# Attention of a hybrid decoder step: P·V as split fp32r passes over the full array, and scores head by head

## Chip, cores and metric

The kernel runs on one core of one Trainium2 chip. The metric is the device time of one execution in microseconds (us), the median of several runs.

## What is computed

One inference step of a two-layer decoder trunk in fp32, for 1024 prompt tokens and 8 sample tokens that share all weights. Layer 0 mixes tokens by sliding-window attention (16 query heads of 64, 4 key/value heads, window 128, a sink per head, rotary positions), layer 1 by chunkwise retention. A gated ConvFFN follows each mixer, with a post-layer norm after each part. The change lies in the attention of layer 0 over the prompt, cut here to its core:

```python
qb = q.reshape(b, nb, WINDOW, ATTN_HEADS, ATTN_HEAD_DIM)          # nb = 8 blocks of 128 tokens
s = jnp.einsum('...qkgd,...skd->...kgqs', qg, k) * (ATTN_HEAD_DIM ** -0.5)   # keys: previous and own block
s = jnp.where(valid, s, -jnp.inf)
m = jnp.maximum(jnp.max(s, axis=-1, keepdims=True), sink)
p = jnp.exp(s - m)
w = p / (jnp.sum(p, axis=-1, keepdims=True) + jnp.exp(sink - m))
o = jnp.einsum('...kgqs,...skd->...qkgd', w, v)
out = o.reshape(b, t, ATTN_HEADS * ATTN_HEAD_DIM) @ w_o
```

## The kernel before

Five engines run five programs, in an order written out by hand; semaphores join them. Large matmuls are done in split fp32r: each fp32 operand x is kept as hi (x rounded to fp32r by ACT's copy) and lo (x − hi, by a subtraction on VectorE or POOL). `accumulate` (L476) then does three passes per term: hi·hi, hi·lo, lo·hi. All 1032 token columns (1024 prompt, 8 sample) stay in SBUF, features on partitions.

Attention runs over four head groups g of one kv head and four query heads (GH=4) each. Within a group TensorE (L643) goes through t = 0 to 8, with a software pipeline over the eight blocks b of 128 tokens:

- `project(t)`: q, k, v of block t, 24 passes of 384 columns into bank t%2 (t = 8 is the sample rows).
- `turn(t-1)`: three transposes of q and k (two heads of q per 128 columns; k is there twice, once per array half) into bank 2.
- `values(t-4)`: P·V into bank 7. Two key blocks (one for block 0) times two head parities, plain fp32; parity 0 writes partitions 0 to 63, parity 1 partitions 64 to 127.
- `scores(t-2)`: q·k into banks 3 and 4. Contraction is over 64, so even heads lie in partitions 0 to 63 and odd heads in 64 to 127. The keys hold a ring of three blocks (KR), so the two key blocks are one piece of 256 columns, except in blocks 3 and 6, where they are two pieces of 128; block 0 has one piece of 128.
- `turn_probs(t-3)`: eight transposes of the probabilities into banks 5 and 6.

The output projection `down(q0, q1)` (L626) follows: 24 jobs q of six passes of 344 columns, added into y by VectorE (`add_y`). For q below 8 the banks alternate (q%2), so job q waits for the add of job q−2; from q=8 there are four banks in groups 0 to 2, and in the last group two until q=16. Between them stand the remaining steps of the pipeline: `down(0,4)`, `values(5)`, `scores(7)`, `turn_probs(6)`, `down(4,8)`, the sample rows' scores, `values(6)`, `turn_probs(7)`, `down(8,12)`, `values(7)`, and so on.

ACT, in each t: `v_in(t)` (copy of v out of the bank), `t_hi(t-1)` (hi of q and k), `heads_hi(t-4)`, `pt_in(t-3)` (copy of the transposed probabilities), `exps(t-2)`. VectorE, in each t: `inverse(t-3)` (L1495), `rope(t)` (L1459 to L1461), `t_lo(t-1)` (L1467), `shift(t-2)` (mask and max, L1482), `heads_lo(t-4)` (L1503). POOL: `probs(t-3)` (L1956, the multiply by the inverse sums), `add_rope(t)`. After the loop VectorE interleaves `add_y` (L1403) with the rest.

What is ordered around the change: `t_hi(t-1)` waits for scores(t-2), since it overwrites q; `turn_probs` waits for POOL's `probs`; `values` waits for `pt_in`; `project(b)` waits for `rope(b-2)`, which frees its bank.

Of the kernel before, what the change touches and what calls it, by code (L numbers as in the profile page):

```python
# [12 lines left out]
P = 128  # L13
# [241 lines left out]
def fillers():  # L255
# [10 lines left out]
    for n in range(NB):  # L266
# [14 lines left out]
ATT_SEMS = ("table_in cache_in rope_t v_in v_fp qk back t_hi t_lo score shifted small small2 expd "  # L281
            "inv probs pt pt_in heads heads_hi heads_lo kv_out win_out s_sc s_scc "
# [39 lines left out]
def build(nc, A):  # L322
    ctx = ExitStack()
    with ctx:
# [45 lines left out]
        K.a_v = sb("a_v", [P, VR, HD])  # L370
# [5 lines left out]
        K.a_pt = sb("a_pt", [P, 2, GH * W])  # L376
# [109 lines left out]
def tensor_engine(pe, K):  # L486
# [36 lines left out]
    def attention(g):  # L523
        last = g == NG - 1

        def project(b):
# [6 lines left out]
            if b >= 2:  # L533
                pe.wait_ge(T["rope_t"], (NB + 1) * g + b - 1)
# [24 lines left out]
        def scores(b):  # L559
# [5 lines left out]
            for j in range(2):  # L565
                q = slice(W * j, W * j + W)
                for k0, at, n in pieces:
                    passes = ((K.a_qh, K.a_kh), (K.a_qh, K.a_kl), (K.a_ql, K.a_kh))
                    for n_pass, (qs, ks) in enumerate(passes):
                        for odd in range(2):  # L570
                            r = slice(HD * odd, HD * odd + HD)
                            mm = pe.matmul(bank[3 + odd][:, j * 256 + at:j * 256 + at + n], qs[r, q], ks[r, k0:k0 + n],
                                           start=(n_pass == 0), stop=(n_pass == 2))
            mm.then_inc(T["score"], 1)

        def turn_probs(b):
            pe.wait_ge(T["probs"], NB * g + b + 1)
            if b >= 1:
                pe.wait_ge(T["pt_in"], NB * g + b)
# [5 lines left out]
        def values(b):  # L585
            pe.wait_ge(T["pt_in"], NB * g + b + 1)
            if b >= 1:
                pe.wait_ge(T["heads_lo"], NB * g + b)
            first = 0 if b else 1
            for t in range(first, 2):  # L590
                for odd in range(2):
                    mm = pe.matmul(bank[7][HD * odd:HD * odd + HD, 0:2 * W], K.a_v[:, (b - 1 + t) % VR, :],  # L592
                                   K.a_pt[:, t, :].rearrange("p (j h n) -> p j h n", j=2, h=2)[:, :, odd, :],
                                   start=(t == first), stop=(t == 1))
            mm.then_inc(T["heads"], 1)
# [15 lines left out]
        def sample_turn_probs():  # L611
# [3 lines left out]
            pe.wait_ge(T["pt_in"], NB * (g + 1))  # L615
# [326 lines left out]
def scalar_engine(act, K):  # L942
# [48 lines left out]
    def attention(g):  # L991
        last = g == NG - 1

        def v_in(b):
            act.wait_ge(S["jobs"], J["qkv", g, b])
            if b < NB:
                after(act, T["heads"], NB * g + max(b - 4, 0))
                act.activation(K.a_v[:, b % VR, :], bank[b % 2][:, 320:384], ACT.Copy).then_inc(T["v_in"], 1)
# [23 lines left out]
        def pt_in(b):  # L1022
# [1382 lines left out]
```

## Time and profile before

| | |
|---|---|
| Time, median of 3 runs | 3007.52 us (3007.17 to 3007.52) |
| The profiled execution's own time | 3007.52 us |
| Its span, first to last instruction | 3005.7 us |
| TensorE busy (matmuls) | 2881.6 us, 96% |
| VectorE busy | 1515.3 us, 50% |
| ACT busy | 901.8 us, 30% |
| POOL busy | 584.5 us, 19% |
| Granted TensorE clock, mean | 0.984 |

PE is TensorE's matmuls, PEld its weight loads (both at once are normal), DVE is VectorE, POOL is GpSimd, SP the engine that issues most DMAs. Matmul ends are modelled, so the distance from one start to the next says more than a duration. "x2" in a timeline merges like instructions that follow each other. In the granted clock 1.00 is 2.4 GHz, 0.50 is 1.2 GHz. "Idle before, releaser" is how long an engine stood ahead of an instruction and who ended it; "issue" means that nothing in the profile shows what it waited for. An fp32 matmul shows as more than one record, an fp32r pass as one.

### The profile page before, as it was taken

To read this page: it belongs to the slowest core of one execution; us is meant where nothing else is said; L and a number is where in the kernel's file an instruction comes from. 1 tells how busy PE (TensorE), PEld (TensorE's weight loads), DVE (VectorE), ACT (ScalarE), POOL (GpSimd) and SP (SyncE) were. 2 spreads that over 40 slices of the span, in tenths; PEclk is the share of its full clock that TensorE was granted. 3 is DMA by queue.
4 is the path that set the end of the run, shared out by engine and by line. 5 is a ranking of instruction groups with operands and counts; after the bars stand their busy time and mean duration, and the time that the engine had idled before them with its cause. 6 is when DMAs were issued, how large, how long until landed. Compare 5 with 4: busy or idle time off the path is not lost.

```text
span 3005.7 us, 44058 instructions
## 1 busy us (share of the span) xinstructions
PE 2881.6 (96%) x17996; PEld 2735.8 (91%) x17996; DVE 1515.3 (50%) x3021; ACT 901.8 (30%) x1683; POOL 584.5 (19%) x496
## 2 busy tenths in 40 slices
PE   6999979999999999999999999999999999999996
PEld 6888859999999999998888888888899999999995
DVE  4555566544454444615344354366675454444445
ACT  4344344222211222322433433322152122222113
POOL 1333351000000003403123232111141000000012
PEclk9999989999999999999999999999999999999997
DMA  3200100211111111234555555666411111111101
GB/s 127 75 30 16 43 30 30 70 43 43 43 55 44 43 57 49 75 124 147 174 182 179 165 180 167 218 197 200 152 43 57 43 51 49 43 57 43 43 25 57
DMA packets 192488, 260.48 MB, mean 87 GB/s; under 512 B 29280, under 2 KB 150752, under 8 KB 192256
## 3 DMA queue, kind: packets, MB, share of 16 engines
q1 hardware_dynamic: 126352, 195.64, 20.6%
q10 hardware_dynamic: 65936, 62.03, 6.0%
q8 instruction: 143, 2.34, 0.3%
q14 instruction: 57, 0.47, 0.1%
HBM read 191.50 MB, written 68.20 MB: 86 GB/s over the span
## 4 chain that ended last, share of the span: by engine, by line
PE 83%; issue 6%; DVE 5%; POOL 3%; ACT 2%; SPq 1%; DMA 0%; ACTq 0%; POOLq 0%; DVEq 0%
PE bank L480 26%; PE bank L482 26%; PE bank L481 26%; PE bank L891 2%; ACT y L983 1%; POOL a_prob L1956 1%; PE bank L592 1%; DVE wl L1378 1%; PE bank L518 1%; DVE bank L1425 1%; PE bank L582 1%; PE bank L857 0%; DVE y L1432 0%; POOL a_qk L1945 0%; DVE n_sq L1418 0%
## 5 line engine op out<-in xcount | busy, mean ns | idle before, releaser
L480 PE MATMUL bank<-xh,wh 128*128 128x344 f32 x3648 | 1182.1, 324 | 29.0 <-DVE wl L1378 10.9
L482 PE MATMUL bank<-xh,wl 128*128 128x344 f32 x3648 | 1169.2, 321 | 0.0
L481 PE MATMUL bank<-xl,wh 128*128 128x344 f32 x3648 | 1169.1, 320 | 0.0
L480 PEld LDWEIGHTS bank<-xh,wh 128*128 128x128 f32 x3648 | 689.5, 189 | 57.6 <-issue 20.5
L481 PEld LDWEIGHTS bank<-xl,wh 128*128 128x128 f32 x3648 | 689.1, 189 | 5.2 <-issue 0.2
L482 PEld LDWEIGHTS bank<-xh,wl 128*128 128x128 f32 x3648 | 689.3, 189 | 0.0
L1403 DVE TENSOR_TENSOR y<-bank,y 128x344 f32<-128x344 f32 x648 | 324.8, 513 | 227.6 <-PE bank L482 227.3
L1998 POOL TENSOR_TENSOR f_hl<-f_cv,f_hh 128x344 fp32r<-128x344 f32 x132 | 122.9, 932 | 1276.7 <-ACT f_hh L1100 1276.7
L480 PE MATMUL bank<-f_hh,wh 128*128 128x344 f32 x1056 | 339.8, 322 | 0.0
L482 PE MATMUL bank<-f_hh,wl 128*128 128x344 f32 x1056 | 337.4, 319 | 0.0
L481 PE MATMUL bank<-f_hl,wh 128*128 128x344 f32 x1056 | 337.1, 319 | 0.0
L1378 DVE TENSOR_TENSOR wl<-raw,wh 128x1024 fp32r<-128x1024 f32 x187 | 226.6, 1240 | 159.3 <-ACT wh L953 159.2
L1086 ACT ACTIVATE f_ab<-bank 128x344 f32<-128x344 f32 x132 | 60.2, 456 | 643.8 <-PE bank L482 643.8
L953 ACT ACTIVATE wh<-raw 128x1024 fp32r<-128x1024 f32 x216 | 218.1, 1048 | 69.5 <-PE bank L482 43.3
L1637 DVE TENSOR_TENSOR f_cv<-f_cv,bank 128x344 f32<-128x344 f32 x132 | 67.5, 512 | 300.1 <-PE bank L482 297.9
L481 PEld LDWEIGHTS bank<-f_hl,wh 128*128 128x128 f32 x1056 | 198.5, 188 | 0.6
L480 PEld LDWEIGHTS bank<-f_hh,wh 128*128 128x128 f32 x1056 | 198.5, 188 | 0.6
L482 PEld LDWEIGHTS bank<-f_hh,wl 128*128 128x128 f32 x1056 | 198.6, 188 | 0.0
L1618 DVE TENSOR_SCALAR f_cv<-f_ab,taps 128x344 f32<-128x344 f32 (+1 forms) x132 | 64.0, 485 | 211.2 <-ACT f_ab L1086 211.2
L1100 ACT ACTIVATE f_hh<-f_cv 128x344 fp32r<-128x344 f32 x132 | 64.8, 491 | 311.6 <-DVE f_cv L1637 311.6
L1173 ACT ACTIVATE p_plain<-bank 128x344 f32<-128x344 f32 x96 | 43.9, 457 | 298.0 <-PE bank L482 279.0
L2036 POOL TENSOR_TENSOR r_sl<-r_state,r_sh 128x1024 fp32r<-128x1024 f32 x28 | 66.8, 2386 | 270.9 <-ACT r_sh L1283 270.9
(202 smaller groups left out, 3509.5 us busy)
## 6 DMA issues: line engine op xcount, KB each, us to landing
raw<-in_w SPq DMA_DIRECT2D x216, 512.0 KB, 3.7
scratch_qkvg<-p_plain ACTq DMA_DIRECT2D x96, 172.0 KB, 2.1
r_s<-in_state_in SPq DMA_DIRECT2D x32, 512.0 KB, 3.6
out_state_s<-r_s ACTq DMA_DIRECT2D x32, 512.0 KB, 5.0
scratch_qkvg<-p_rot ACTq DMA_DIRECT2D x24, 344.0 KB, 2.9
r_cxq<-scratch_qkvg SPq DMA_DIRECT2D x32, 256.0 KB, 5.6
r_cxv<-scratch_qkvg SPq DMA_DIRECT2D x32, 256.0 KB, 5.7
r_cxg<-scratch_qkvg SPq DMA_DIRECT2D x32, 256.0 KB, 5.2
```

The source lines that it names most:

```text
L480: pe.matmul(out, ah, bh, start=(k == 0), stop=False)
L481: pe.matmul(out, ah, bl, start=False, stop=False)
L482: mm = pe.matmul(out, al, bh, start=False, stop=(k == n - 1))
L953: act.activation(K.wh[:, SLOT[s], :], K.raw[:, s % RAW, :], ACT.Copy).then_inc(S["hi_done"], 1)
L1086: act.activation(K.ab[:, t % 3, 2 + ch * CH:2 + (ch + 1) * CH], bank[BANK["up", L, t, 0, ch]][:, 0:CH], ACT.Copy)\
L1100: act.activation(K.hh[:, t // 2 % 2, t % 2, columns(ch)], K.cv[:, cv_of(t, ch), :], ACT.Copy).then_inc(S["h_hi"], 1)
L1378: dve.tensor_tensor(K.wl[:, SLOT[s], :], K.raw[:, s % RAW, :], K.wh[:, SLOT[s], :].bitcast(F32), ALU.subtract)\
L1403: dve.tensor_tensor(t, bank[b][:, 0:CH], t, ALU.add).then_inc(S["yadd"], 1)
L1618: x = dve.tensor_scalar(v[:, 0:m], a[:, c0:c0 + m], tap(0), tap(3), ALU.mult, ALU.add)
L1637: dve.tensor_tensor(v, v, bank[BANK["up", L, t, 1, ch]][:, 0:CH], ALU.mult).then_inc(S["gate"], 1)
L1998: pool.tensor_tensor(K.hl[:, t // 2 % 2, t % 2, columns(ch)], v, k.bitcast(F32), ALU.subtract).then_inc(S["h_lo"], 1)
L2036: pool.tensor_tensor(K.sl[:, :, :], K.state[:, :, :], K.sh[:, :, :].bitcast(F32), ALU.subtract).then_inc(R["s_lo"], 1)
```

## The change

P·V becomes a sum of three fp32r products over the full array: ACT's copies `v_hi` and `pt_hi` now write the hi parts (v twice side by side, so that 128 weight columns fill both halves of bank 7), and VectorE makes the lo parts, `v_lo` at the end of `rope` and `pt_lo` as a new step. The result has 512 columns, of which heads_hi and heads_lo read the halves that hold each parity. `scores` now takes head after head, the three passes of a head in a row, in place of alternating even and odd heads within each pass. `project(b)` waits for v_lo (`v_free`) instead of rope's last operation. pt_lo stands last in each t on VectorE, and in the output projection after shift(7) (for block 6) and after sample_shift (for block 7).

```diff
--- before.py
+++ after.py
@@ -367,13 +367,15 @@
         K.sq = sb("n_sq", [P, KT, CH])
 
         sb = place(REGION)
-        K.a_v = sb("a_v", [P, VR, HD])
+        K.a_vh = sb("a_vh", [P, VR, 2, HD], F32R)
+        K.a_vl = sb("a_vl", [P, VR, 2, HD], F32R)
         K.a_vf = sb("a_vf", [P, HD])
         K.a_vs = sb("a_vs", [NS, HD])
         K.a_qk = sb("a_qk", [P, 2, 384])
         K.a_prob = sb("a_prob", [P, GH, 2 * W])
         K.a_st = sb("a_st", [P, 8, GH])
-        K.a_pt = sb("a_pt", [P, 2, GH * W])
+        K.a_pth = sb("a_pth", [P, 2, GH * W], F32R)
+        K.a_ptl = sb("a_ptl", [P, 2, GH * W], F32R)
         K.a_oh = sb("a_oh", [P, 2, TOK], F32R)
         K.a_ol = sb("a_ol", [P, 2, TOK], F32R)
         K.a_sq = sb("a_sq", [HD, 5, NS])
@@ -531,7 +533,7 @@
             if g == 0:
                 pe.wait_ge(S["x_lo"], 1 + sum((b + 1) * W > end for _, end in PIECES[:-1]))
             if b >= 2:
-                pe.wait_ge(T["rope_t"], (NB + 1) * g + b - 1)
+                pe.wait_ge(T["v_free"], NB * g + b - 1)
             o = bank[b % 2][0:m, 0:384].rearrange("m (a n) -> m a n", a=3)
             t = slice(b * W, b * W + m)
             terms = []
@@ -562,37 +564,32 @@
                 pe.wait_ge(T["shifted"], GH * (NB * g + b))
             kb = b % KR * W
             pieces = [(kb, W, W)] if b == 0 else [(kb - W, 0, 2 * W)] if b % KR else [((KR - 1) * W, 0, W), (0, W, W)]
-            for j in range(2):
-                q = slice(W * j, W * j + W)
+            for h in range(GH):
+                r = slice(HD * (h % 2), HD * (h % 2) + HD)
+                q = slice(W * (h // 2), W * (h // 2) + W)
                 for k0, at, n in pieces:
-                    passes = ((K.a_qh, K.a_kh), (K.a_qh, K.a_kl), (K.a_ql, K.a_kh))
-                    for n_pass, (qs, ks) in enumerate(passes):
-                        for odd in range(2):
-                            r = slice(HD * odd, HD * odd + HD)
-                            mm = pe.matmul(bank[3 + odd][:, j * 256 + at:j * 256 + at + n], qs[r, q], ks[r, k0:k0 + n],
-                                           start=(n_pass == 0), stop=(n_pass == 2))
+                    o = bank[3 + h % 2][:, (h // 2) * 256 + at:(h // 2) * 256 + at + n]
+                    mm = accumulate(pe, o, [(K.a_qh[r, q], K.a_ql[r, q], K.a_kh[r, k0:k0 + n], K.a_kl[r, k0:k0 + n])])
             mm.then_inc(T["score"], 1)
 
         def turn_probs(b):
             pe.wait_ge(T["probs"], NB * g + b + 1)
             if b >= 1:
-                pe.wait_ge(T["pt_in"], NB * g + b)
+                pe.wait_ge(T["pt_lo"], NB * g + b)
             for t in range(0 if b else 1, 2):
                 for h in range(GH):
                     mm = pe.transpose(bank[5 + t][:, h * W:(h + 1) * W], K.a_prob[:, h, t * W:(t + 1) * W], ident[:, :])
             mm.then_inc(T["pt"], 1)
 
         def values(b):
-            pe.wait_ge(T["pt_in"], NB * g + b + 1)
+            pe.wait_ge(T["pt_lo"], NB * g + b + 1)
             if b >= 1:
                 pe.wait_ge(T["heads_lo"], NB * g + b)
-            first = 0 if b else 1
-            for t in range(first, 2):
-                for odd in range(2):
-                    mm = pe.matmul(bank[7][HD * odd:HD * odd + HD, 0:2 * W], K.a_v[:, (b - 1 + t) % VR, :],
-                                   K.a_pt[:, t, :].rearrange("p (j h n) -> p j h n", j=2, h=2)[:, :, odd, :],
-                                   start=(t == first), stop=(t == 1))
-            mm.then_inc(T["heads"], 1)
+            terms = []
+            for t in range(0 if b else 1, 2):
+                v = b - 1 + t
+                terms.append((K.a_vh[:, v % VR, :, :], K.a_vl[:, v % VR, :, :], K.a_pth[:, t, :], K.a_ptl[:, t, :]))
+            accumulate(pe, bank[7][:, :], terms).then_inc(T["heads"], 1)
 
         def sample_scores():
             pe.wait_ge(T["t_lo"], (2 * NB + 1) * (g + 1))
...
@@ -991,11 +988,12 @@
     def attention(g):
         last = g == NG - 1
 
-        def v_in(b):
+        def v_hi(b):
             act.wait_ge(S["jobs"], J["qkv", g, b])
             if b < NB:
                 after(act, T["heads"], NB * g + max(b - 4, 0))
-                act.activation(K.a_v[:, b % VR, :], bank[b % 2][:, 320:384], ACT.Copy).then_inc(T["v_in"], 1)
+                act.activation(K.a_vh[:, b % VR, :, :], bank[b % 2][:, 320:384].rearrange("m (a n) -> m a n", a=1)
+                               .to_broadcast([P, 2, HD]), ACT.Copy).then_inc(T["v_hi"], 1)
             if b == NB - 1:
                 after(act, T["kv_out"], 64 * g)
                 act.activation(K.a_vf[:, :], bank[b % 2][:, 320:384], ACT.Copy).then_inc(T["v_fp"], 1)
@@ -1019,12 +1017,12 @@
                                accum_out=K.a_st[:, 4, h:h + 1])
             act.activation(K.a_st[:, 5, :], K.a_st[:, 3, :], ACT.Exp).then_inc(T["expd"], 1)
 
-        def pt_in(b):
+        def pt_hi(b):
             act.wait_ge(T["pt"], NB * g + b + 1)
             after(act, T["heads"], NB * g + b)
             for t in range(0 if b else 1, 2):
-                a = act.activation(K.a_pt[:, t, :], bank[5 + t][:, :], ACT.Copy)
-            a.then_inc(T["pt_in"], 1)
+                a = act.activation(K.a_pth[:, t, :], bank[5 + t][:, :], ACT.Copy)
+            a.then_inc(T["pt_hi"], 1)
 
         def heads_hi(b):
             act.wait_ge(T["heads"], NB * g + b + 1)
@@ -1033,18 +1031,18 @@
             for h in range(2):
                 r = slice(HD * h, HD * h + HD)
                 a = act.activation(K.a_oh[r, :, b * W:(b + 1) * W],
-                                   bank[7][r, 0:2 * W].rearrange("p (j n) -> p j n", j=2), ACT.Copy)
+                                   bank[7][r, :].rearrange("p (j h n) -> p j h n", j=2, h=2)[:, :, h, :], ACT.Copy)
             a.then_inc(T["heads_hi"], 1)
 
         for t in range(NB + 2):
             if t <= NB:
-                v_in(t)
+                v_hi(t)
             if t >= 1:
                 t_hi(t - 1)
             if t >= 4:
                 heads_hi(t - 4)
             if t >= 3:
-                pt_in(t - 3)
+                pt_hi(t - 3)
             if t >= 2:
                 exps(t - 2)
 
...
@@ -1447,7 +1445,7 @@
         def rope(b):
             m = P if b < NB else NS
             if b < NB:
-                dve.wait_ge(T["v_in"], NB * g + b + 1)
+                dve.wait_ge(T["v_hi"], NB * g + b + 1)
             if b >= NB - 1:
                 dve.wait_ge(T["v_fp"], 2 * g + b - NB + 2)
             after(dve, T["qk"], 2 * (NB + 1) * g + (2 * (b - 1) if b >= 2 else 0))
@@ -1460,6 +1458,10 @@
             dve.tensor_tensor(a2[:, :, 1, :], src[:, :, 0, :], sn.to_broadcast([m, 5, 32]), ALU.mult)
             dve.scalar_tensor_tensor(a2[:, :, 0, :], src[:, :, 1, :], -1.0, sn.to_broadcast([m, 5, 32]),
                                      ALU.mult, ALU.mult).then_inc(T["rope_t"], 1)
+            if b < NB:
+                dve.tensor_tensor(K.a_vl[:, b % VR, :, :], bank[b % 2][:, 320:384].rearrange("m (a n) -> m a n", a=1)
+                                  .to_broadcast([P, 2, HD]), K.a_vh[:, b % VR, :, :].bitcast(F32),
+                                  ALU.subtract).then_inc(T["v_free"], 1)
 
         def t_lo(b):
             if b < NB:
@@ -1496,12 +1498,18 @@
             dve.wait_ge(T["small2"], NB * g + b + 1)
             dve.reciprocal(K.a_st[:, 7, :], K.a_st[:, 6, :]).then_inc(T["inv"], 1)
 
+        def pt_lo(b):
+            dve.wait_ge(T["pt_hi"], NB * g + b + 1)
+            for t in range(0 if b else 1, 2):
+                a = dve.tensor_tensor(K.a_ptl[:, t, :], bank[5 + t][:, :], K.a_pth[:, t, :].bitcast(F32), ALU.subtract)
+            a.then_inc(T["pt_lo"], 1)
+
         def heads_lo(b):
             dve.wait_ge(T["heads_hi"], NB * g + b + 1)
             for h in range(2):
                 r = slice(HD * h, HD * h + HD)
                 a = dve.tensor_tensor(K.a_ol[r, :, b * W:(b + 1) * W],
-                                      bank[7][r, 0:2 * W].rearrange("p (j n) -> p j n", j=2),
+                                      bank[7][r, :].rearrange("p (j h n) -> p j h n", j=2, h=2)[:, :, h, :],
                                       K.a_oh[r, :, b * W:(b + 1) * W].bitcast(F32), ALU.subtract)
             a.then_inc(T["heads_lo"], 1)
 
@@ -1564,18 +1572,22 @@
                 shift(t - 2)
             if t >= 4:
                 heads_lo(t - 4)
+            if t >= 3:
+                pt_lo(t - 3)
         t_lo(NB)
         add_y(0, 2)
         inverse(NB - 2)
         add_y(2, 4)
         heads_lo(NB - 3)
         shift(NB - 1)
+        pt_lo(NB - 2)
         add_y(4, 6)
         inverse(NB - 1)
         add_y(6, 8)
         sample_copy()
         heads_lo(NB - 2)
         sample_shift()
+        pt_lo(NB - 1)
         add_y(8, 10)
         sample_probs()
         add_y(10, 12)
```

What is left out renames semaphores in the same way (`v_in` to `v_hi`, `pt_in` to `pt_hi` and `pt_lo`).

## Rows read from the trace of the kernel before

**Rows 1.** The page: the span, and the chain of waits by engine.
```profile
span 3005.7 us, 44058 instructions
...
PE 83%; issue 6%; DVE 5%; POOL 3%; ACT 2%; SPq 1%; DMA 0%; ACTq 0%; POOLq 0%; DVEq 0%
```

**Rows 2.** Busy time by stretch, second group: PE, PEld, DVE, ACT, POOL, clock, DMA.
```profile
115.00:208.00 93.00, 89.18 (x629) 78.55 (x630) 47.73 (x192) 40.42 (x134) 33.84 (x30) 0.98 0.13 47
```

**Rows 3.** TensorE's waits, same group: total us, times, longest.
```profile
PE bank L582 <- POOL a_prob L1956: 1.4, 3, 0.8
PE bank L480 <- DVE y L1403: 1.3, 2, 0.9
```

**Rows 4.** Timeline, TensorE, one block: start, duration, what; PEld is its weight load.
```profile
157.29 0.49 PE L552 MATMUL bank<-ident,a_qk 128*128 128x128 f32 x3
157.71 1.08 PE L592 MATMUL bank<-a_pt,a_v 128*64 128x256 f32 x8
...
158.72 0.19 PEld L572 LDWEIGHTS bank<-a_kh,a_qh 64*128 64x128 f32 x2 [0.38 <-issue]
...
158.88 0.28 PE L572 MATMUL bank<-a_kl,a_qh 64*128 64x128 f32 x2
...
160.00 0.28 PE L572 MATMUL bank<-a_kh,a_ql 64*128 64x128 f32 x2
```

**Rows 5.** Timeline, TensorE, first and last of the 12 passes of one run.
```profile
72.47 0.34 PE L480 MATMUL bank<-wh,xh 128*128 128x384 f32 x1
...
74.39 0.34 PE L482 MATMUL bank<-wh,xl 128*128 128x384 f32 x1
```

**Rows 6.** Timeline, TensorE, scores of block 7: two passes with their loads.
```profile
191.50 0.18 PEld L572 LDWEIGHTS bank<-a_kh,a_qh 64*128 64x128 f32 x2 [0.39 <-issue]
...
191.72 0.28 PE L572 MATMUL bank<-a_kl,a_qh 64*128 64x256 f32 x2
...
192.20 0.29 PE L572 MATMUL bank<-a_kh,a_ql 64*128 64x256 f32 x2
...
192.41 0.31 PEld L582 LDWEIGHTS bank<-ident,a_prob 128*128 128x128 f32 x3
```

**Rows 7.** Groups by line, VectorE: count, busy us, mean ns, idle before.
```profile
L1403 DVE TENSOR_TENSOR y<-bank,y 128x344 f32<-128x344 f32 x648 | 324.8, 513 | 227.6 <-PE bank L482 227.3
L1378 DVE TENSOR_TENSOR wl<-raw,wh 128x1024 fp32r<-128x1024 f32 x187 | 226.6, 1240 | 159.3 <-ACT wh L953 159.2
...
L1467 DVE TENSOR_TENSOR a_ql<-bank,a_qh 128x256 fp32r<-128x256 f32 x32 | 13.5, 423 | 40.0 <-ACT a_kh L1011 40.0
```

**Rows 8.** Timeline from the end of scores to the next probabilities.
```profile
151.08 0.28 PE L572 MATMUL bank<-a_kh,a_ql 64*128 64x256 f32 x2
...
152.04 0.42 DVE L1467 TENSOR_TENSOR a_ql<-bank,a_qh 128x256 fp32r<-128x256 f32 x1 [1.06 <-ACT a_kh L1011]
...
154.42 0.85 DVE L1503 TENSOR_TENSOR a_ol<-bank,a_oh 64x256 fp32r<-64x256 f32 x2
...
156.75 0.16 DVE L1495 TENSOR_TENSOR a_st<-a_st 128x4 f32<-128x4 f32 x1 [1.47 <-ACT a_st L1020]
...
157.20 1.89 POOL L1956 TENSOR_TENSOR a_prob<-a_prob,a_st 128x1024 f32<-128x1024 f32 x1 [4.00 <-DVE a_st L1497]
```

**Rows 9.** Timeline, VectorE and TensorE, two places of the output projection.
```profile
187.83 0.94 DVE L1403 TENSOR_TENSOR y<-bank,y 128x344 f32<-128x344 f32 x2
...
188.40 0.43 PE L480 MATMUL bank<-a_oh,wh 128*128 128x344 f32 x1 [0.89 <-DVE y L1403]
...
192.48 0.86 DVE L1503 TENSOR_TENSOR a_ol<-bank,a_oh 64x256 fp32r<-64x256 f32 x2 [1.37 <-ACT a_oh L1035]
...
195.22 0.93 DVE L1403 TENSOR_TENSOR y<-bank,y 128x344 f32<-128x344 f32 x2
...
195.78 0.42 PE L480 MATMUL bank<-a_oh,wh 128*128 128x344 f32 x1 [0.37 <-DVE y L1403]
```

**Rows 10.** Busy time of a stretch, columns as in rows 2 (clock 0.50 is 1.2 GHz).
```profile
200.60:203.90 3.30, 3.30 (x16) 2.29 (x13) 1.13 (x3) 1.46 (x4) 1.60 (x1) 0.50 0.24 32
```

More of the change, by code:

```diff
@@ L280 @@
         "p_in prod rot plain out_r0 out_r1 out_p0 out_p1").split()
-ATT_SEMS = ("table_in cache_in rope_t v_in v_fp qk back t_hi t_lo score shifted small small2 expd "
-            "inv probs pt pt_in heads heads_hi heads_lo kv_out win_out s_sc s_scc "
+ATT_SEMS = ("table_in cache_in rope_t v_hi v_fp v_free qk back t_hi t_lo score shifted small small2 expd "
+            "inv probs pt pt_hi pt_lo heads heads_hi heads_lo kv_out win_out s_sc s_scc "
             "s_tr s_mx s_ex s_p s_pt s_ptc s_o s_of s_oh s_ol dchain").split()
@@ L614, in sample_turn_probs @@
             pe.wait_ge(T["s_p"], g + 1)
-            pe.wait_ge(T["pt_in"], NB * (g + 1))
+            pe.wait_ge(T["pt_lo"], NB * (g + 1))
             pe.transpose(bank[5][:, 0:32], K.a_sp[:, 0:W], ident[0:32, 0:32])
@@ L1058, in attention @@
         heads_hi(NB - 2)
-        pt_in(NB - 1)
+        pt_hi(NB - 1)
         split_next(1)
```

## The prediction

> **What bounds the kernel now.** I read the page first: which engine the chain of waits goes through, and how long the execution is [rows 1]. TensorE has 83% of that chain. Then I asked where the change sits. Everything it touches runs in the attention of layer 0, four head groups of about 93 us each, so I took the busy table of one group: 89.2 us of TensorE work in 93.0 us, VectorE only 47.7 us [rows 2]. So in attention, too, a microsecond of TensorE work is nearly a microsecond of time, and about 3.8 us per group is standing still. The list of waits of TensorE in that group says where it stands: 1.4 us for the POOL multiply that writes a_prob, and 1.3 us for VectorE's adds into y [rows 3]. VectorE is half idle on average, but it must be read where TensorE waits for it, below.
>
> **Part 1: P·V (values).** Before, a block does four fp32 matmuls of 64 weight columns and 256 moving columns, two per key block; the two head parities write the two halves of the bank and run beside each other. The trace shows them as 8 records. After, there are six fp32r passes of 128 weight columns and 512 moving columns (three products for each of two key blocks), each filling the array. The rows of one block [rows 4]: from the first of the three q/k transposes at 157.29 to the first weight load of scores at 158.72 is 1.43 us. What does a 512-column pass cost? The trace has none. The 384-column passes of the projection start at 72.47 and 74.39 with 11 steps between, 0.1745 us each [rows 5]; at the granted 2.4 GHz 384 columns stream in 0.160, so 0.0145 is overhead. Then 512 columns take 0.213+0.0145=0.228 us. Bounds: 0.213 (streaming alone) and 0.233 (0.1745 scaled by 512/384). After, the same stretch is three transposes at 0.11 (0.33; the step of 128 columns in the same rows), five steps of 0.228 (1.14), and the last pass with the change to the half-array form. From the last 256-column pass of scores to the next load in full form, 192.20 to 192.41, is 0.21 [rows 6], which is 0.107 of streaming and 0.10 of switch, so 0.213+0.10=0.31. Sum 1.78, or +0.35 per block; for 28 blocks +9.8. Block 0 of each group has one key block and pays about 0.1, +0.3 for four. Together **+10.1**.
>
> **Part 2: scores.** Matmul count and sizes stay; their order changes. Before, even and odd heads alternate: even heads lie in array rows 0 to 63, odd ones in rows 64 to 127, and each pair starts together (one row "x2") every 0.12 us for 256 columns: 191.72 to 192.20 is four steps [rows 6]. With 128 columns a step is 0.112 (158.88 to 160.00, ten steps [rows 4]), which is the weight load's own pace. After, a head's three passes follow each other in the same rows, so they can't share the array. Only where a head changes can the last pass of one head and the first of the next, in the other half, run together: 12 passes take 9 steps in place of 6, and 24 passes (blocks 3 and 6, whose keys lie in two pieces) 21 in place of 12. Taken: blocks 1, 2, 4, 5, 7: +3×0.12=+0.36; blocks 3, 6: +9×0.112=+1.0; block 0: +3×0.112=+0.34. Block 7's part is swallowed by a VectorE chain (part 3). So 16×0.36+8×1.0+4×0.34=**+15.2**. Bounds: no sharing at head changes gives 6, 12 and 6 more steps, +24.9; below, out-of-order pairing would give 0, for which no row speaks, since matmuls start in program order in every row.
>
> A harder case is that a load and a stream in the same half exclude each other. Then a step costs 0.112+0.107=0.22 us with 256 columns and 0.112+0.053=0.165 with 128: 16×(9×0.22−6×0.12)+8×(21×0.165−12×0.112)+4×(9×0.165−6×0.112) is +40 in place of 15.2. The rows speak against it: before, the next loads already go to the very halves that are streaming, and the 256-column step is still 0.12, not 0.22 [rows 6]. The Trainium skill ("TensorE: Matmul & The Clock Gate", Part 3, The mechanism) states this rule, that a weight load overlaps running matmuls only when the row group differs; by it the sum would be 58, by the rows 33. The trace so far disagrees with it.
>
> **Part 3: VectorE's new work.** pt_lo subtracts 128x512 out of PSUM, two per block. Nearest rows: 513 ns for 128x344 and 423 ns for 128x256, both PSUM subtract/add [rows 7]; the slope of 1.02 ns per column gives 0.69 for 512. Neighbouring operations overlap by some 0.08, so a pair is 1.3 us (bounds 1.15 and 1.45). v_lo (128x128) is about 0.28.
> In the block loop both are covered. rope's v_lo falls in VectorE's wait for a_kh, which is 1.06 us in block 2 [rows 8]. pt_lo follows the heads_lo pair: that starts at 154.42, takes 0.85, then pt_lo to 156.6; VectorE's next operation, waiting for the exps, starts at 156.75 [rows 8]. Cover 0.17 us a block; without it each 0.1 late comes 0.1 later at the POOL multiply, which starts TensorE's probability transposes. There TensorE, itself slower by 0.7, has slack. PV waits for pt_lo, but project and turn (over 4 us) stand between. v_hi writes 128 instead of 64 columns, some 0.05 on ACT ahead of rope, hidden by the same slack. The projection of block b now waits for v_lo of block b−2, one short operation later than before and a whole block early; the transposes of P wait for pt_lo of the block before, done over 4 us earlier. No DMA moves, and the queues of SP and POOL keep their order.
> In the output projection that follows, pt_lo isn't covered. Job q=2 waits for VectorE's add of q=0: adds start at 187.83 and the matmul at 188.40 after 0.89 us idle [rows 9]. The new order puts pt_lo(5) straight ahead of this add, after shift(6) and heads_lo(4), which already are late: +1.3. Again at q=6: heads_lo(5) from 192.48, shift(7), then the adds at 195.22, the matmul at 195.78 after 0.37 idle [rows 9]. pt_lo(6) goes between shift and adds: +1.3. This chain starts at heads_hi, before scores(7) ends, so the +0.36 of scores(7) disappears in it. Four groups: 8×1.3=+10.4. pt_lo(7) precedes add_y(8,10): in the last group q=10 uses a bank of q=8 and stands some 0.9 longer; in the others q=8 to 11 have four banks. **+11.3**. Bounds: 0 if these adds are still in time, 8×1.45+1.5=13.1.
>
> **Part 4: what comes back.** TensorE's three waits for a_prob (1.4 us a group, 0.8 the longest [rows 3]) have a fixed length measured from scores' end: from 151.08 to 157.20+1.89=159.09 [rows 8]. With 0.36 more in scores, and 0.35 in PV from block 1 on, two vanish and 0.4 of the longest stays: −1.0 a group, **−4.0**. One stretch of 3.3 us is at 1.2 GHz (200.6 to 203.9 at 0.50 [rows 10]), one like it in each group, and it holds part of one P·V: its surplus counts about twice there, **+0.8**.
>
> Sum: 10.1+15.2+11.3−4.0+0.8=+33.4. The profiled execution took 3007.52 us (span 3005.7), which is the median, so 3007.5+33.4=3040.9: **3041 us**, 1.1% slower. Its own range is 3036 to 3047.
>
> **Rivals.**
> - Passes of one head never share with the next head: +24.9 for scores in place of 15.2, 3051. For it: I have no row in which halves change after a same-half run. Against: loads and matmuls of different halves start within one row everywhere.
> - VectorE's pt_lo costs nothing in the output projection: 3041−11=3030. For it: average load of 50%. Against: TensorE already stands waiting for exactly these adds.
> - More falls of the clock. The granted clock fell to 1.2 GHz after the short sample-score matmuls that follow the 0.37 us stand at q=6, and the stand at q=2 grows to 2.2 us. A fall like the present one costs 1.7 us (3.3 us at half, and its edges); one more per group gives 3048.
> - Not slower: the end is set by the ring scores → max → exp → sum → POOL multiply → transposes and not by TensorE, which would just wait less. Place: the wait ahead of the probability transposes. It decides only where TensorE stands there by 0.7 us or more in each of 28 blocks; the rows show three waits of 1.4 us in all per group. If it did: 3007.5, no change.
> - VectorE becomes a bound in the loop too: pt_lo at 1.24 us each, what 128x1024 takes at L1378 [rows 7], makes a pair 1.1 us longer; 0.7 of it runs beside TensorE's own surplus, so 28×0.4, and 8×1.1 in the output projection: +20 over mine, 3061. Against: the rate per column of the rows of PSUM.
> - Loads and streams of one half exclude each other (part 2): 3066.
>
> **How the numbers follow.** Forecast 0.50, no sharing 0.16, free adds 0.12, clock falls 0.08, ring (no change) 0.04, VectorE loop 0.03, loads excluded by streams 0.04, and 0.03 for a gain whose cause I don't see. The range takes the free-adds case with the low pass bound (28×6×0.015=2.5 less) at the bottom, 3026, and no-sharing with clock falls at the top, 3057. 0.2% (6 us) is about what can be told from no change: slower 0.93, within 0.04, faster 0.03.
>
> **What would show each step.** L592's successor: six 512-column passes 0.228 apart, about 1.4 us where 8 records took 1.01. Scores: 1.27 us where a block took 0.91 (191.50 to 192.41 [rows 6]), and 1.0 us more in blocks 3 and 6, with loads of both halves starting together only at head changes. pt_lo rows of 0.69. Idle ahead of q=2 near 2.2 and ahead of q=6 near 1.7, released by y. Waits for a_prob nearly gone. TensorE busy per group up by about 6, span of a group by about 8.3. Wrong would be: adds in time, a pass step over 0.25, or scores unchanged.

## The result, and the profile after

The changed kernel takes 3030.47 us in the median (3027.41 to 3033.03), the kernel before 3007.52: ratio 1.0077, 95% interval 1.0058 to 1.0094. The forecast was 3041 with a range of 3026 to 3057. It is slower, as forecast, by 23 us where 33 were forecast, and the time lies below the narrower range of 3036 to 3047 that the prediction gave for its own case. The profiled execution took 3027.81 us.

The page of the profile of the changed kernel, against [rows 1]: the chain is still TensorE's to 83%, VectorE's part is up from 5% to 6%.

```profile
span 3026.0 us, 44030 instructions
...
PE 83%; DVE 6%; issue 4%; ACT 3%; POOL 2%; DMA 1%; SPq 1%; ACTq 0%; POOLq 0%; DVEq 0%
```

Busy time from one group's last P·V to that of the next: length, then PE, PEld, DVE, ACT, POOL, granted clock, DMA. First the kernel before (groups 2, 3 and 4):

```profile
109.17:207.70 98.53, 94.67 (x672) 83.17 (x671) 51.90 (x205) 42.45 (x138) 36.45 (x32) 0.98 0.17 58
207.70:306.18 98.48, 94.67 (x672) 83.48 (x671) 51.56 (x207) 42.47 (x138) 36.21 (x31) 0.98 0.11 34
306.18:403.15 96.97, 93.14 (x672) 82.17 (x672) 51.23 (x203) 42.47 (x138) 35.86 (x31) 1.00 0.11 34
```

Then the changed kernel:

```profile
113.14:215.30 102.16, 96.52 (x659) 87.02 (x657) 61.81 (x228) 42.81 (x138) 36.24 (x32) 1.00 0.16 56
215.30:317.50 102.20, 96.53 (x659) 87.01 (x657) 61.85 (x228) 42.80 (x138) 36.24 (x32) 1.00 0.10 33
317.50:420.90 103.40, 96.79 (x658) 86.99 (x657) 62.94 (x232) 42.80 (x138) 36.67 (x32) 1.00 0.10 32
```

Two things are to be seen. A group is 3.6 to 6.4 us longer. And the granted clock of groups 2 and 3 rose from 0.98 to 1.00: the stretch at 1.2 GHz that each of these groups had is absent from this execution. The group before without it (96.97) is the fair one to compare: 5.2 us more for a middle group, of which 3.4 are TensorE's busy time, and 6.4 for the last.

TensorE's waits in one group, against [rows 3]: those for y grew from 1.3 to 3.5 us, those for a_prob shrank from 1.4 to 1.0.

```profile
PE bank L482 <- DVE y L1401: 3.5, 2, 2.0
PE bank L581 <- POOL a_prob L1968: 1.0, 2, 0.7
```

The block of [rows 4], in the changed kernel's timeline (start, duration, what):

```profile
161.69 0.49 PE L554 MATMUL bank<-ident,a_qk 128*128 128x128 f32 x3
161.94 0.48 PE L482 MATMUL bank<-a_pth,a_vh 128*128 128x512 f32 x1
162.25 0.39 PE L483 MATMUL bank<-a_ptl,a_vh 128*128 128x512 f32 x1
...
163.18 0.39 PE L484 MATMUL bank<-a_pth,a_vl 128*128 128x512 f32 x1
163.49 0.32 PE L482 MATMUL bank<-a_kh,a_qh 64*128 64x128 f32 x1
163.66 0.27 PE L483 MATMUL bank<-a_kl,a_qh 64*128 64x128 f32 x1
163.77 0.27 PE L484 MATMUL bank<-a_kh,a_ql 64*128 64x128 f32 x1
163.78 0.38 PE L482 MATMUL bank<-a_kh,a_qh 64*128 64x128 f32 x2
163.94 0.32 PE L483 MATMUL bank<-a_kl,a_qh 64*128 64x128 f32 x2
...
164.73 0.32 PE L484 MATMUL bank<-a_kh,a_ql 64*128 64x128 f32 x2
164.84 0.27 PE L482 MATMUL bank<-a_kh,a_qh 64*128 64x128 f32 x1
...
165.26 1.09 PE L581 MATMUL bank<-ident,a_prob 128*128 128x128 f32 x8
```

From the transposes to scores is now 1.80 us, the four steps from 162.25 to 163.18 are 0.2325 each: forecast 1.78 and 0.228. Scores takes 1.77 (163.49 to 165.26); before, it took 1.49, from 158.72 [rows 4] to the next transposes at 160.21; 2.5 was forecast. It starts with three single passes, ends with three, and has nine pairs ("x2") between: 15 steps, not 21. And a block with one piece of 256 keys:

```profile
172.21 0.39 PE L482 MATMUL bank<-a_kh,a_qh 64*128 64x256 f32 x2
172.44 0.29 PE L483 MATMUL bank<-a_kl,a_qh 64*128 64x256 f32 x2
172.55 0.29 PE L484 MATMUL bank<-a_kh,a_ql 64*128 64x256 f32 x2
172.68 0.28 PE L482 MATMUL bank<-a_kh,a_qh 64*128 64x256 f32 x2
...
173.13 1.09 PE L581 MATMUL bank<-ident,a_prob 128*128 128x128 f32 x8
```

That is six pairs and 0.92 us, as in [rows 6]. In the program the two L482 passes of the first pair are the first and the fourth matmul: TensorE ran the fourth beside the first.

VectorE's new work, by line (count, busy us, mean ns), against [rows 7]: 684 ns for 512 columns, forecast 690.

```profile
L1504 DVE TENSOR_TENSOR a_ptl<-bank,a_pth 128x512 fp32r<-128x512 f32 x60 | 38.7, 684 | 0.6
...
L1462 DVE TENSOR_TENSOR a_vl<-bank,a_vh 128x128 fp32r<-128x128 f32 x32 | 9.0, 281 | 0.0
```

The first place of [rows 9], with pt_lo between heads_lo and the adds:

```profile
192.84 0.85 DVE L1511 TENSOR_TENSOR a_ol<-bank,a_oh 64x256 fp32r<-64x256 f32 x2
...
193.72 1.29 DVE L1504 TENSOR_TENSOR a_ptl<-bank,a_pth 128x512 fp32r<-128x512 f32 x2
195.03 0.92 DVE L1401 TENSOR_TENSOR y<-bank,y 128x344 f32<-128x344 f32 x2
...
195.58 0.42 PE L482 MATMUL bank<-a_oh,wh 128*128 128x344 f32 x1 [1.95 <-DVE y L1401]
```

TensorE stands 1.95 us there instead of 0.89. At the second place it is 1.56 instead of 0.37:

```profile
204.52 0.42 PE L482 MATMUL bank<-a_oh,wh 128*128 128x344 f32 x1 [1.56 <-DVE y L1401]
```

### The profile page after: what moved, and what is told of

It is laid out like the page before. It is cut to its first block, busy times and chain, and to the rows that moved or that the text cites. A ratio compares the mean times of both kernels' runs of the same rounds, so it can differ in the third digit from the quotient of the medians.

```text
span 3026.0 us, 44030 instructions
## 1 busy us (share of the span) xinstructions
PE 2893.7 (96%) x17936; PEld 2753.6 (91%) x17936; DVE 1558.9 (52%) x3113; ACT 903.3 (30%) x1683; POOL 583.9 (19%) x496
## 4 chain that ended last, share of the span: by engine, by line
PE 83%; DVE 6%; issue 4%; ACT 3%; POOL 2%; DMA 1%; SPq 1%; ACTq 0%; POOLq 0%; DVEq 0%
PE bank L482 27%; PE bank L484 26%; PE bank L483 26%; PE bank L888 1%; ACT y L980 1%; DVE bank L1423 1%; PE bank L581 1%; DVE wl L1376 1%; PE bank L520 1%; DVE y L1430 1%; ACT xh L984 0%; PE bank L854 0%; DMA raw<-in_w 0%; DVE n_sq L1416 0%; DVE xl L1438 0%
## 5 line engine op out<-in xcount | busy, mean ns | idle before, releaser
L482 PE MATMUL bank<-xh,wh 128*128 128x344 f32 x3648 | 1181.1, 324 | 30.3 <-DVE wl L1376 10.9
L482 PEld LDWEIGHTS bank<-xh,wh 128*128 128x128 f32 x3648 | 688.7, 189 | 59.1 <-issue 21.1
L482 PE MATMUL bank<-f_hh,wh 128*128 128x344 f32 x1056 | 339.8, 322 | 0.0
L482 PEld LDWEIGHTS bank<-f_hh,wh 128*128 128x128 f32 x1056 | 198.5, 188 | 0.6
```

Source lines behind the costliest of these rows:

```text
L482: pe.matmul(out, ah, bh, start=(k == 0), stop=False)
```

## Experiments

Two theories stand against each other on scores. The forecast's: in the new order the two halves of the array work at the same time only where the head changes. The new one, **look-ahead**: TensorE starts a pass of the other half before its turn when it lies up to three matmuls ahead of the oldest one not yet started. On the rest: P·V costs its passes, and VectorE's lo work costs what it delays the adds.

Single times scatter by up to 12 us for one kernel, in step with the execution's mean granted clock (0.987 with 3001.7, 0.981 with 3013.6 for the kernel before). Straight lines through all runs, with one slope for all and a height for each kernel, give 1.75 us less for each 0.001 of clock more. So beside each median stands the difference to the kernel before at equal clock, by that slope; it is good to a microsecond or two. It takes out the clock even where the change itself had moved it, so it is the cost of the work and the waits, and the median is what the change did to the time.

| kernel | median, us | ratio, 95% interval | at equal clock |
|---|---|---|---|
| changed kernel | 3030.5 | 1.0077 (1.0058 to 1.0094) | +21.0 |
| s_heads | 3007.7 | 1.0002 (0.9993 to 1.0011) | +1.5 |
| s_even_first | 3017.5 | 1.0025 (1.0015 to 1.0036) | +10.2 |
| s_piece | 3005.7 | 0.9997 (0.9988 to 1.0006) | −0.1 |
| lo_only | 3020.7 | 1.0035 (1.0021 to 1.0049) | +10.3 |
| lo_short | 3018.6 | 1.0040 (1.0027 to 1.0054) | +11.4 |
| lo_late | 3016.6 | 1.0033 (1.0022 to 1.0044) | +11.2 |
| pv_lo | 3026.1 | 1.0062 (1.0050 to 1.0074) | +18.5 |
| pv_two | 3021.9 | 1.0044 (1.0032 to 1.0057) | +10.9 |
| after_first | 3014.6 | 1.0020 (1.0011 to 1.0029) | +7.2 |
| adds_first | 2996.1 | 0.9962 (0.9949 to 0.9974) | −8.8 |

**s_heads**: the kernel before with the changed scores only (what is left out is the old loop, with the passes outside and odd inside).

```diff
-            for j in range(2):
-                q = slice(W * j, W * j + W)
+            for h in range(GH):
+                r = slice(HD * (h % 2), HD * (h % 2) + HD)
+                q = slice(W * (h // 2), W * (h // 2) + W)
                 for k0, at, n in pieces:
...
+                    o = bank[3 + h % 2][:, (h // 2) * 256 + at:(h // 2) * 256 + at + n]
+                    mm = accumulate(pe, o, [(K.a_qh[r, q], K.a_ql[r, q], K.a_kh[r, k0:k0 + n], K.a_kl[r, k0:k0 + n])])
```

> The kernel before with nothing but the new order of scores (head after head). Look-ahead theory: TensorE starts a pass of the other half up to three matmuls ahead of its turn, so 12 passes still take 6 steps and only the two-piece blocks 3 and 6 get longer, by the 0.28 us seen in the changed kernel: 8 x 0.28 = +2.2, less a little waiting for a_prob, 3009 to 3010. Rival, as forecast (halves share only where the head changes): 9 and 21 steps, +15.2, less up to 4 of waiting: 3018 or more.

Measured 3007.7, +1.5 at equal clock, and the ratio's interval ends at 1.0011, 3.3 us. The forecast's +11 or more is excluded; look-ahead fits, though the median lies 1.3 below what it was to give. Its last group has no stretch at 1.2 GHz, and so compares with the 96.97 of the kernel before without any correction for the clock:

```profile
304.94:402.66 97.72, 93.84 (x672) 82.74 (x672) 52.03 (x205) 42.50 (x138) 36.18 (x32) 1.00 0.12 34
```

That is 0.75 us a group, or 3.0 in four.

**s_even_first**: the loop of s_heads with another order of heads (shown against s_heads).

```diff
-            for h in range(GH):
+            for h in (0, 2, 1, 3):
```

> The kernel before with scores head by head in the order 0, 2, 1, 3: both even heads, then both odd ones. Look-ahead of three matmuls: the odd half starts only three matmuls before the even half ends, so 9 steps for 12 passes and 21 for 24: 16 x 0.35 + 8 x 1.0 + 4 x 0.34 = +15, less some 4 of waiting for a_prob: 3018.5 (3016 to 3021). No limit on the look-ahead: 3007.5, nothing changes. Sharing only at a change of half: 11 and 23 steps, +21.7 less 4.5: 3025.

Measured 3017.5, +10.2 at equal clock. A look-ahead without limit (0) is out, and 3025 too; 3016 to 3021 was the expectation for three matmuls. The timeline shows the limit itself, a block with 256 keys:

```profile
169.40 0.38 PE L480 MATMUL bank<-a_kh,a_qh 64*128 64x256 f32 x1
169.62 0.28 PE L481 MATMUL bank<-a_kl,a_qh 64*128 64x256 f32 x1
169.74 0.28 PE L482 MATMUL bank<-a_kh,a_ql 64*128 64x256 f32 x1
169.74 0.39 PE L480 MATMUL bank<-a_kh,a_qh 64*128 64x256 f32 x2
169.96 0.29 PE L481 MATMUL bank<-a_kl,a_qh 64*128 64x256 f32 x2
170.08 0.29 PE L482 MATMUL bank<-a_kh,a_ql 64*128 64x256 f32 x2
170.20 0.28 PE L480 MATMUL bank<-a_kh,a_qh 64*128 64x256 f32 x1
170.32 0.28 PE L481 MATMUL bank<-a_kl,a_qh 64*128 64x256 f32 x1
170.44 0.28 PE L482 MATMUL bank<-a_kh,a_ql 64*128 64x256 f32 x1
```

The odd half's first pass is the seventh matmul. It starts at 169.74, right after the third has started and the fourth is next: three ahead. So nine steps, and in the blocks of two pieces 21: there the odd half starts at 161.34, right after the ninth of the even half's twelve passes. These are the step counts that the forecast had for scores, and they cost 10.2: what was wrong in the forecast was the count for the changed order, not the price of a step.

The rows also settle whether weight loads and streams of one half exclude each other. From 169.62 to 169.74, and from 170.20 to 170.44, one half runs alone, and its steps are still 0.12 us for 256 columns, so loading and streaming in the same half do overlap, as [rows 6] had said. The Trainium skill ("TensorE: Matmul & The Clock Gate", Part 3, The mechanism) states that a weight load overlaps running matmuls only when the row group differs; this trace disagrees. The same section of the Trainium skill says that matmuls start in strict program order; the pairs above disagree.

**s_piece**: head by head, but the two halves never more than three matmuls apart.

```diff
             for j in range(2):
...
                 for k0, at, n in pieces:
...
+                    for odd in range(2):
+                        r = slice(HD * odd, HD * odd + HD)
+                        o = bank[3 + odd][:, j * 256 + at:j * 256 + at + n]
+                        mm = accumulate(pe, o, [(K.a_qh[r, q], K.a_ql[r, q], K.a_kh[r, k0:k0 + n], K.a_kl[r, k0:k0 + n])])
```

> The kernel before with scores head by head, but for each piece of keys the even and then the odd head, so that the two halves are never more than three matmuls apart. Look-ahead theory: 6 and 12 steps as before, 3007.5. Sharing only at head changes: 9 and 17 steps, +11.6 less about 3 of waiting: 3016.

Measured 3005.7, −0.1 at equal clock. The order of passes costs nothing as long as the partner lies within the look-ahead.

**lo_only**: the kernel before, with VectorE's new work added and nobody reading its results (v_lo, the places of the calls and the other renamed waits are left out here).

```diff
...
+        def pt_lo(b):
+            dve.wait_ge(T["pt_in"], NB * g + b + 1)
+            for t in range(0 if b else 1, 2):
+                a = dve.tensor_tensor(K.a_ptl[:, t, :], bank[5 + t][:, :], K.a_pt[:, t, :], ALU.subtract)
+            a.then_inc(T["pt_lo"], 1)
...
-            pe.wait_ge(T["pt_in"], NB * g + b + 1)
+            pe.wait_ge(T["pt_lo"], NB * g + b + 1)
```

> The kernel before (P.V in plain fp32, old order of scores) with VectorE's new work added at the same places and with the same waits: pt_lo and v_lo are computed, nothing reads their results. VectorE theory: the waits of TensorE for the adds of q=0 and q=4 grow by 1.1 each as in the changed kernel, plus 0.9 at q=10 of the last group: 4 x 2.25 + 0.9 = +9.9, 3017.4. Rival: these waits come from the longer P.V passes and not from VectorE's work: 3007.5.

Measured +10.3 at equal clock, 3020.7 in the median. TensorE's waits in the second group, where P·V is as short as before:

```profile
PE bank L482 <- DVE y L1405: 3.5, 2, 1.9
PE bank L584 <- POOL a_prob L1973: 1.4, 3, 0.8
```

The 3.5 us for y are there without the longer P·V (1.3 in [rows 3]), so they are VectorE's.

**lo_short**: the changed kernel with 8 columns of pt_lo in place of 512. The second product reads hi of P once more, so the number and size of the passes stay, and the lo part of P is left out of the sum.

```diff
-                terms.append((K.a_vh[:, v % VR, :, :], K.a_vl[:, v % VR, :, :], K.a_pth[:, t, :], K.a_ptl[:, t, :]))
+                terms.append((K.a_vh[:, v % VR, :, :], K.a_vl[:, v % VR, :, :], K.a_pth[:, t, :], K.a_pth[:, t, :]))
...
-                a = dve.tensor_tensor(K.a_ptl[:, t, :], bank[5 + t][:, :], K.a_pth[:, t, :].bitcast(F32), ALU.subtract)
+                a = dve.tensor_tensor(K.a_ptl[:, t, 0:8], bank[5 + t][:, 0:8], K.a_pth[:, t, 0:8].bitcast(F32), ALU.subtract)
```

> The changed kernel with pt_lo cut to 8 of 512 columns; the second product takes hi of P in place of lo, so the lo part of P is left out of the computation, at the same number and size of passes. VectorE theory: the waits for the adds of q=0 and q=4 fall back to 0.9 and 0.4, and the 0.9 in the last group goes: 4 x 2.25 + 0.9 = 9.9 less than the changed kernel, about 3020.5 against 3030.5; what remains over the kernel before is P.V. If P.V's passes made the waits, they stay and so does the time, 3030.

Measured 3018.6: 12 less than the changed kernel, 9.6 less at equal clock, as against 9.9. What is left, +11.4, is P·V and the order of scores; with the +1.5 of s_heads taken off, P·V is 9.9. Parts and whole agree: 9.9+1.5+10.3=21.7, measured +21.0. lo_short still runs v_lo and the 8 columns, as lo_only does, so the parts overlap by a little.

A middle group without a stretch at 1.2 GHz, and its waits for y:

```profile
212.09:312.12 100.03, 96.48 (x659) 86.97 (x658) 54.26 (x228) 42.83 (x138) 35.82 (x32) 1.00 0.11 33
PE bank L482 <- DVE y L1401: 1.4, 2, 0.9
```

So the group lengths give the same split without any line through clocks: from 96.97 to 97.72 the order of scores, 0.75; to 100.03 P·V, 2.3; to 102.20 VectorE, 2.2. In four groups that is 3.0, 9.2 and 8.7, and VectorE has about 1 more in the last group.

**lo_late**: pt_lo behind the adds.

```diff
-            if t >= 3:
+            if 3 <= t < NB:
                 pt_lo(t - 3)
...
         add_y(0, 2)
+        pt_lo(NB - 3)
...
         shift(NB - 1)
+        add_y(4, 6)
         pt_lo(NB - 2)
-        add_y(4, 6)
...
         sample_shift()
+        add_y(8, 10)
         pt_lo(NB - 1)
-        add_y(8, 10)
```

> The changed kernel with pt_lo of blocks 5, 6 and 7 behind the pair of adds that it stood ahead of; same work in another order. VectorE theory: the adds are in time again, and P.V of blocks 5 to 7 starts late enough to find its lo part: about 9 to 10 less than the changed kernel, 3021. Rival: the wait only moves to P.V, which now waits for pt_lo: 3028 to 3030.

Measured 3016.6, 9.8 less at equal clock. The waits for y are back at 1.3 us a group, and P·V doesn't wait in their place:

```profile
PE bank L482 <- DVE y L1401: 1.3, 2, 0.9
```

Nearly all of VectorE's cost was its place in the order.

**pv_lo**: the changed kernel with the old scores.

> The changed kernel with the old order of scores. Look-ahead theory: 8 x 0.28 less in scores, 3028 to 3029. Rival, as forecast: 15 less, 3015.

Measured 3026.1, 2.5 less at equal clock (4.4 less in the medians, more than expected): neither 0 nor 15. With s_heads the order of scores is worth 1.5 to 3.

**pv_two**: the changed kernel without the third product, so lo of v is left out of the sum.

```diff
-            accumulate(pe, bank[7][:, :], terms).then_inc(T["heads"], 1)
+            for k, (ah, al, bh, bl) in enumerate(terms):
+                pe.matmul(bank[7][:, :], ah, bh, start=(k == 0), stop=False)
+                mm = pe.matmul(bank[7][:, :], ah, bl, start=False, stop=(k == len(terms) - 1))
+            mm.then_inc(T["heads"], 1)
```

> The changed kernel without the third product of P.V (lo of v times hi of P is left out of the computation), so four passes in place of six in 28 blocks and two in place of three in four. If P.V costs its passes at 0.23 us each: 28 x 0.46 + 4 x 0.23 = 13.8 less than the changed kernel, 3016.7, and a block's P.V is then 0.08 shorter than the plain fp32 one. If something else makes P.V longer (the switch of form, waits for lo): clearly less than 10 comes off, 3021 or more.

Measured 3021.9 in the median, the value named for "something else", but at equal clock 10.1 less. The missing part shows in its waits: those for a_prob rose from 1.0 to 1.6 us a group, 2.4 in all, which with 10.1 is 12.5 of the 13.8.

```profile
PE bank L482 <- DVE y L1404: 3.5, 2, 1.9
PE bank L581 <- POOL a_prob L1971: 1.6, 3, 0.9
```

The rest of the median goes with the clock: its runs had 0.981 to 0.984. Why this kernel is granted less isn't settled, so this run supports the price of a pass but doesn't show it alone.

**adds_first**: the kernel before with VectorE reordered.

```diff
-            if t >= 4:
+            if 4 <= t < NB:
                 heads_lo(t - 4)
         t_lo(NB)
         add_y(0, 2)
+        heads_lo(NB - 4)
...
-        heads_lo(NB - 3)
         shift(NB - 1)
         add_y(4, 6)
+        heads_lo(NB - 3)
```

> The kernel before with VectorE's heads_lo of block 4 behind the adds of q=0 and 1, and heads_lo of block 5 behind shift(7) and the adds of q=4 and 5. If VectorE's place in the order sets TensorE's waits for these adds (0.89 and 0.37 a group), the first falls to almost nothing and the second goes: 4 x (0.85 + 0.37) = 4.9 less, 3002.5. If not: 3007.5.

Measured 2996.1, ratio 0.9962, which beats both kernels. One group, columns as above:

```profile
201.77:297.28 95.51, 92.89 (x672) 82.18 (x671) 52.02 (x205) 42.34 (x138) 36.19 (x32) 1.00 0.11 35
```

The direction was right and the size forecast for it (4.9) too small. The waits of 1.26 a group are gone; against a group without a clock stretch (97.02 in s_piece) it is 1.51 shorter. The 0.25 beyond the waits fits the passes that restart after a stand: their rows have 0.42 and 0.43 us [rows 9], where the passes behind them have 0.32. That makes 6.0. Against the groups of the kernel before at 98.5 it is 3.0, since none of its groups had a stretch at 1.2 GHz. The other 2.8 of the −8.8 aren't accounted for. Part of them may be clock: a stretch at 1.2 GHz makes a group 1.5 us longer (98.5 against 97.0), while by the 1.75 us per 0.001 a stretch of 3.3 us takes 1.0 off (an estimate: it lowers the mean over 3000 us by 0.00055), so three missing stretches would leave 1.5 that the line doesn't cover.

**after_first**: lo_late with heads_lo moved as well.

> The changed kernel with all of VectorE's lo work of blocks 4 to 6 behind the adds (lo_late, and heads_lo of blocks 4 and 5 moved as in adds_first). VectorE theory: the waits for the adds of q=0 and q=4 go in full, 4 x 1.26 = 5.0 less than lo_late (3016.6), and P.V of block 5 may wait 0.5 for its lo part: 3012 to 3014; less by up to 5 if the falls of the clock go too, as they did in adds_first. It stays above adds_first (2996.1) by what P.V costs, 11 to 12, plus that wait: 3008 to 3014. If moving work on VectorE were worth nothing here: 3016.6.

Measured 3014.6, just above the 3012 to 3014 expected, and +7.2 at equal clock: 4.0 less than lo_late, though the medians differ by only 2.0. The waits for y are gone but for the one between groups, 0.7, and a new wait for pt_lo stands ahead of P·V, as expected:

```profile
PE bank L482 <- DVE a_ptl L1504: 0.6, 1, 0.6
```
Over adds_first it is 16 at equal clock: P·V's 10, 2.6 of that wait, 1.5 of scores, and 2 within the error.

## Why the prediction came out as it did

- **P·V, +10.1**: right. A block's stretch is 1.80 where 1.78 was forecast, +0.37 a block and with block 0 some 10.7 in all; a pass takes 0.2325, the upper bound of the forecast's 0.213 to 0.233, where 0.228 was taken. 9.9 by lo_short and s_heads, or 9.2 by the group lengths, is what is left when the waits that it gave back (below) are off. The prediction says that the trace before has no 512-column pass. It has, in the retention of layer 1, and a VectorE row of pt_lo's very form; they give 0.23 us a pass and 688 ns, where it worked its way to 0.228 and 690 from smaller ones:

```profile
1360.28 0.39 PE L480 MATMUL bank<-r_vh,r_kdh 128*128 128x512 f32 x1
1360.51 0.40 PE L481 MATMUL bank<-r_vl,r_kdh 128*128 128x512 f32 x1
1360.74 0.39 PE L482 MATMUL bank<-r_vh,r_kdl 128*128 128x512 f32 x1
L1763 DVE TENSOR_TENSOR r_vl<-bank,r_vh 128x512 fp32r<-128x512 f32 x32 | 22.0, 688 | 33.5 <-ACT r_vh L1218 33.5
```

- **Scores, +15.2**: the step that failed, and in its mechanism: halves that share only at head changes. That gave 21 and 9 steps; the trace has 15 and 6. Measured are +1.5 at equal clock and 3.0 by the group lengths. The forecast did name the lower bound of 0, and put it aside "since matmuls start in program order in every row". Those rows couldn't tell: in the old program the partner was always the next matmul, so program order and look-ahead look alike.
- **VectorE in the output projection, +11.3**: right in place and size. 10.3 by lo_only. The wait at q=2 grew by 1.06 and at q=6 by 1.19 where 1.3 each was forecast, and the last group paid about 1 more.
- **VectorE in the block loop, nothing**: right. lo_only adds no wait there, and a_prob's stay at 1.4.
- **Waits that come back, −4.0**: 0.4 a group came back, 1.6 in all, and P·V brought it: the waits for a_prob are 1.4 us a group in s_heads and 1.0 in lo_short. The other 2.4 would have needed longer scores; in s_even_first, which has them, these waits fall to 0.8. So scores stood in the forecast for 15.2−2.4=12.8, and 10 to 11 of that didn't come, which is the whole surplus of 10.4.
- **Clock, +0.8**: not tested. The profiled execution lacks the stretch at 1.2 GHz in groups 2 and 3, which takes some 1.5 us off each, and the forecast had not foreseen that. Over all runs the mean clock is 0.9836 for the changed kernel and 0.9843 for the kernel before, 1.3 us by the line: the forecast's sign, but within the scatter. At equal clock the change costs 21.0, in the medians 23.0.
- **Rivals**: no sharing at all (3051) and loads excluded by streams (3066) fell with the pairs and the single passes. Free adds named 3030, which is the very time measured, and is wrong all the same: lo_only charges 10.3 for the adds. That the time agrees is chance, since scores fell short by about as much as the adds cost. The time is in the range only because the low end, 3026, had been set by this rival. More clock falls came true in lo_only (two stretches in each of groups 1 to 3), not in the changed kernel's profile. The ring as the bound and VectorE as the bound of the loop fell too: scores, P·V and VectorE each have a price of their own, and the waits for a_prob stay at 1.0.
- **Its own signs**: "scores unchanged" was one of three that it had named for being wrong, and in six blocks of eight that is what the trace has. TensorE's busy time per group rose by 3.4 where 6 was named, and a middle group is 5.2 longer where 8.3 was. The stands of 1.95 and 1.56 came close to the 2.2 and 1.7 named.

By its steps: 10.1+11.3 came nearly as forecast, 15.2−4.0 should have been about 1.5 with 1.6 of waits coming back, and 21 to 23 follows.

## What to carry over

In these kernels the order of small matmuls in two array halves mattered only when partners were more than three matmuls apart: keep them within that and write the loop as is easiest. A trace in which partners are always neighbours says nothing about what happens when they aren't, so a bound argued from it should keep its chance. And ask of each new operation on a half-idle engine what it is put in front of: the same pt_lo cost 10 us ahead of the adds and almost nothing behind them, and moving two old operations the same way made the kernel before faster.

## What the runs showed of the hardware

- TensorE starts matmuls of the other array half out of program order, up to three matmuls ahead of the oldest not yet started (pairs from 172.21 on; single passes up to 163.77 and, in s_even_first, 169.74).
- A half that runs alone takes 0.12 us per 256-column pass (170.20 to 170.44 in s_even_first) and 0.11 per 128-column pass (from 164.84 on in the changed kernel), weight load included, the same as both halves together.
- A 512-column fp32r pass takes 0.2325 us at 2.4 GHz (162.25 to 163.18), and six of them take longer than the four plain fp32 matmuls that they replace: 0.37 us a block.
- The mean granted clock of an execution varies from 0.981 to 0.987 for one and the same kernel, and 0.001 of it goes with 1.75 us. One stretch at 1.2 GHz makes a group of the kernel before 1.5 us longer (98.5 against 97.0), and such stretches appear at different places from run to run. What decides whether one follows a stand of TensorE remains open: adds_first has none in its groups 2 to 4, lo_only two in each of groups 1 to 3.
